# Hybrid attention and RWKV kernel, one core: attention of layer 0 interleaved with its z, u and output projections, values as matmul weights in two column halves, probabilities divided in place

## What is computed

```python
def _even_mixer(h, w_in, w_out, sgu_norm_g, sgu_w, sgu_b):
    B, S, _ = h.shape
    proj = h @ w_in
    q, k, v, u, z = jnp.split(proj, [WIDTH_A, 2 * WIDTH_A, 3 * WIDTH_A, 3 * WIDTH_A + WIDTH_B], axis=-1)
    heads = lambda t: t.reshape(B, S, N_HEADS_A, HEAD_DIM)
    o_a = _dilated_attention(heads(q), heads(k), heads(v)).reshape(B, S, WIDTH_A)
    o_b = _spatial_gating(u, z, sgu_norm_g, sgu_w, sgu_b)
    return jnp.concatenate([o_a, o_b], axis=-1) @ w_out
```

## Time and profile before

| | us |
|---|---|
| median of 3 runs (lowest to highest) | 1554.79 (1551.72 to 1555.05) |
| the profiled execution | 1548.98 |
| its span, first to last instruction | 1547.0 |
| TensorE busy | 1336.6 (86%) |
| VectorE busy | 671.6 (43%) |
| ScalarE busy | 357.6 (23%) |
| GpSimd busy | 254.8 (16%) |
| mean granted TensorE clock | 0.923 of full speed |

### The profile page before, as it was taken

The page is one execution under the profiler, slowest core; times in us unless marked ns, Lnnn a source line. Parts: engine busy times, 40 slices in busy tenths (PEclk is TensorE's granted clock), DMA queues, the critical chain, the costliest instruction groups (busy, mean ns, idle before and its releaser), DMA issues.

```text
span 1547.0 us, 23213 instructions
## 1 busy us (share of the span) xinstructions
PE 1336.6 (86%) x8816; PEld 811.9 (52%) x8816; DVE 671.6 (43%) x1373; ACT 357.6 (23%) x806; POOL 254.8 (16%) x263
## 2 busy tenths in 40 slices
PE   0899979997799994699999799999999895999990
PEld 0444557756344441343443688888887454444440
DVE  6426434564133233805026556666763324232324
ACT  1100035102111111101048433333332102211111
POOL 1000037000010012100001423444431200100102
PEclk9999867897899997799999899999997997899995
DMA  8649655373599995311110000000001313699975
GB/s 312 205 143 353 205 191 191 129 252 118 183 348 372 355 355 207 127 55 55 55 54 1 29 3 3 19 2 3 3 2 48 116 55 123 206 344 350 372 274 203
DMA packets 128997, 248.35 MB, mean 161 GB/s; under 512 B 8352, under 2 KB 78192, under 8 KB 128912
## 3 DMA queue, kind: packets, MB, share of 16 engines
q1 hardware_dynamic: 116816, 203.09, 37.9%
q0 software_dynamic: 7344, 26.74, 4.7%
q10 hardware_dynamic: 4752, 17.30, 2.7%
HBM read 219.33 MB, written 27.79 MB: 160 GB/s over the span
## 4 chain that ended last, share of the span: by engine, by line
PE 81%; DVE 8%; issue 4%; DMA 3%; ACT 2%; POOL 1%; POOLq 0%; DVEq 0%; SPq 0%; ACTq 0%
PE PS L1905 15%; PE PS L1723 11%; PE PS L1715 9%; PE PS L1922 7%; PE PS L1767 7%; PE PS L2049 2%; PE PS L2065 2%; PE PS L1894 2%; PE PS L2019 2%; PE PS L2071 2%; PE PS L1698 2%; PE PS L1954 2%; DMA arena<-in_ada_w 2%; PE PS L2104 1%; PE PS L1839 1%
## 5 line engine op out<-in xcount | busy, mean ns | idle before, releaser
L1905 PE MATMUL PS<-WR,arena 128*128 (+1 forms) x528 | 238.8, 606 | 11.3 <-ACT arena L1036 6.2
L1723 PE MATMUL PS<-arena,WR 128*128 128x512 f32 x384 | 168.0, 597 | 3.4 <-ACT arena L970 3.4
L1905 PEld LDWEIGHTS PS<-WR,arena 128*128 128x128 f32 x528 | 99.7, 194 | 128.5 <-issue 124.3
L1715 PE MATMUL PS<-WR,arena 128*128 128x512 f32 x320 | 143.1, 607 | 3.8 <-DVE arena L1478 3.8
L1723 PEld LDWEIGHTS PS<-arena,WR 128*128 128x128 f32 x384 | 73.3, 192 | 96.4 <-issue 92.8
L1922 PE MATMUL PS<-W,arena 128*128 x264 | 119.0, 593 | 3.9 <-DVE arena L1412 3.9
L1207 DVE SCALAR_TENSOR_TENSOR arena<-arena,cact 128x1024 f32<-128x1024 f32 x77 | 98.8, 1283 | 36.5 <-DMA arena<-in_ada_w 31.8
L1767 PE MATMUL PS<-WR,arena 128*128 128x512 f32 x256 | 112.2, 595 | 0.0
L1401 DVE TENSOR_TENSOR arena<-arena,PS 128x256 f32<-128x256 f32 x33 | 13.9, 421 | 212.1 <-ACT arena L1049 191.1
L1715 PEld LDWEIGHTS PS<-WR,arena 128*128 128x128 f32 x320 | 61.6, 195 | 83.2 <-issue 76.3
L796 POOL TENSOR_TENSOR LO<-GB,tmp 128x256 f32<-128x256 f32 x80 | 71.0, 906 | 100.6 <-DVE GB L1540 72.6
(11 more groups left out here) (321 smaller groups left out, 2062.3 us busy)
## 6 DMA issues: line engine op xcount, KB each, us to landing
WR<-in_moe_w SPq DMA_DIRECT2D x66, 1024.0 KB, 7.5
arena<-in_ada_w SPq DMA_DIRECT2D x96, 512.0 KB, 5.2
W<-in_moe_w SPq DMA_DIRECT2D x33, 1024.0 KB
expert_rows<-arena ACTq DMA_DIRECT2D x33, 512.0 KB, 7.2
WR<-in_rwkv_w_rkv SPq DMA_DIRECT2D x6, 2048.0 KB, 7.9
WR<-in_mix_w_in SPq DMA_DIRECT2D x5, 2048.0 KB, 10.6
WR<-in_mix_w_out SPq DMA_DIRECT2D x2, 2048.0 KB, 8.1
expert_rows<-arena SPq DMA_DIRECT2D x1, 4096.0 KB, 14.3
```

Of the source, the lines that this page charges most:

```text
L1715: last = mm(out, act_T[:, c, b * P:(b + 1) * P], WR[:, tile % 2, c, :], start=(c == 0), stop=(c == KC - 1))
L1723: last = mm(out, WR[:, tile % 2, c, f * P:(f + 1) * P], act_T[:, c, :], start=(c == 0), stop=(c == KC - 1))
L1905: last = mm(PS[:, 2, :], XgT[:, c, :], WR[:, slot, c, :].rearrange("p s f -> p (s f)"), start=(c == 0), stop=(c == KC - 1))
```

## The change

- **Order on TensorE.** z and u are no longer projected ahead of attention. One block of z comes ahead of the scores of rounds 0, 2, 4 and 6, one block of u ahead of those of rounds 8, 10, 12 and 14. Tiles are loaded in the order q, k, v, z, u. mod(2) is in round 6, the transposes of the gating weights in round 8, the mixing products in rounds 10 to 13, the transposes of their result in rounds 12 to 15. In round 16 come gate(0) and the first unit of the output projection, in round 17 the second, in round 18 mod(3); `out_proj` goes on from the third.
- **Values as weights.** A pair's output is now made with V as weights (64 columns) and the transposed probabilities as moving operand (128 columns), the even head on the lower half of the columns, the odd head on the upper. The result has features on partitions, so the transposes `oT` (L1857) and their copies are gone; VectorE copies the bank to `OT0` (in the area LO), and `sT` goes to `ST0`, where z was.
- **Divided in place.** VectorE makes the reciprocals of a pair's denominators one round later and multiplies the pair's two rows of probabilities by them before they are transposed.
- **Ada steps.** VectorE does 2 instead of 3 steps behind each block of v, one at the head of rounds 0 to 3, two in each of rounds 6 to 17, so all 24 of L = 2; GpSimd does none. SP loads the second output tile behind all chunks of L = 2.
- ScalarE's gelu (and the sum of z's squares) comes ahead of the exps of every even round.

```diff
+MOD2_AT, SWT_AT, MIX_AT = 6, 8, 10
...
-        tiles = [(io["mix_w_in"][0], n * 512) for n in range(5)] + [(io["mix_w_out"][0], n * 512) for n in range(2)]
-        tile_last = [("q", 3), ("k", 3), ("v", 3), ("u", 3), ("z", 3), ("y", 3), ("y", 7)]
+        tiles = [(io["mix_w_in"][0], n * 512) for n in (0, 1, 2, 4, 3)] + [(io["mix_w_out"][0], n * 512) for n in range(2)]
+        tile_last = [("q", 3), ("k", 3), ("v", 3), ("z", 3), ("u", 3), ("y", 3), ("y", 7)]
...
             tile(6)
-            for m in range(12, 3 * KC):
-                ada(2, m)
             sp.wait_ge(*free("u", 4))
             sp.wait_ge(*free("k", 4))
             sp.wait_ge(*free("q", 4))
@@ -670,7 +681,7 @@
                                  ).then_inc(M("w2_in"), 16)
 
...
-            for c in range(KC):
-
-                n = 2 * 3 * KC + 2 * KC + c
-                a, part = acc[:, 2 * D:3 * D], aring[:, n % 4, :]
-                gp.wait_ge(sem(f"ada_in{n % 4}"), 16 * (n // 4 + 1))
-                if c == 0:
-                    gp.wait_ge(*full("mod", 3))
-                    gp.wait_ge(sem("ada_step"), n)
-                    gp.tensor_scalar(a, part, cact[:, 0:1], None, ALU.mult).then_inc(sem("ada_step"), 1)
-                else:
-                    link(gp.tensor_scalar(part, part, cact[:, c:c + 1], None, ALU.mult))
-                    gp.wait_ge(sem("ada_step"), n)
-                    gp.tensor_tensor(a, a, part, ALU.add).then_inc(sem("ada_step"), 1)
 
...
-                               ).then_inc(drained["swT"], 1)
+            def gelu(n):
+
+                if n < NPAIR // 2:
+                    b = n // 2
+                    act.wait_ge(*full("z", b + 1))
+                    nc.scalar.activation(Z0[:, b, :], bank("z", b), ACT.Gelu).then_inc(drained["z"], 1)
+                    act.wait_ge(*free("z", b + 1))
+                    nc.scalar.activation(GB[:, 0:WA], Z0[:, b, :], ACT.Square, accum_out=ss[:, b:b + 1]
+                                         ).then_inc(sem("zss_ready"), 1)
+                else:
+                    b = n // 2 - NB
+                    act.wait_ge(*full("u", b + 1))
+                    nc.scalar.activation(U0[:, b, :], bank("u", b), ACT.Gelu).then_inc(drained["u"], 1)
+
             for n in range(NPAIR + 3):
+                if n < NPAIR and n % 2 == 0:
+                    gelu(n)
...
-                some_ada(3)
-            mod(2)
-            some_ada(12)
-
-            rms(1, sem("zss_ready"), 4, WA)
-            v.wait_ge(sem("gz_in"), 16)
+                some_ada(2)
 
             for n in range(NPAIR + 3):
-                if NB < n <= 2 * NB:
-                    b = n - NB - 1
+                if n < 4:
+                    some_ada(1)
+                if n == MOD2_AT:
+                    mod(2)
+                if n == MIX_AT - 2:
+                    rms(1, sem("zss_ready"), 4, WA)
+                    v.wait_ge(sem("gz_in"), 16)
+                if n == NPAIR - 1:
+                    diag(0, 0)
+                if 0 <= n - MIX_AT - 1 < NB:
+                    b = n - MIX_AT - 1
...
+                if 0 <= n - MIX_AT + 2 < NB:
+                    k = n - MIX_AT + 2
+                    stt(Z0[:, k, :], Z0[:, k, :], rstd[:, k:k + 1], gz, ALU.mult, ALU.mult).then_inc(sem("zn"), 1)
+                if MOD2_AT <= n < MOD2_AT + 3 * KC // 2:
+                    some_ada(2)
...
+                if 1 <= n <= NPAIR:
+                    i = (n - 1) // PPB
+                    k = 2 * (n - 1)
+                    two = slice(k % NHA, k % NHA + 2)
+                    v.wait_ge(sem("probs"), k + 2)
+                    link(nc.vector.reciprocal(rden[:, i % 2, two], den[:, i % 2, two]))
+                    for h in range(2):
+                        row = Pb[:, (k + h) % 6, 0:(i + 1) * P]
+                        ts(row, row, rden[:, i % 2, k % NHA + h:k % NHA + h + 1], None, ALU.mult
+                           ).then_inc(sem("rden"), 1)
                 if n >= 3 and (n - 3) % PPB == PPB - 1:
                     i = (n - 3) // PPB
-                    v.wait_ge(sem("probs"), NHA * (i + 1))
-                    nc.vector.reciprocal(rden[:, i % 2, :], den[:, i % 2, :]).then_inc(sem("rden"), 1)
-                    v.wait_ge(sem("rden"), i + 1)
                     v.wait_ge(sem("pv"), NHA * (i + 1))
-                    if i >= 2:
-                        v.wait_ge(*full("oT", i - 1))
-                    tt(OB[:, i % 2, :].rearrange("p (h d) -> p h d", h=NHA),
-                       bank("o", i).rearrange("p (h d) -> p h d", h=NHA),
-                       rden[:, i % 2, :].unsqueeze(2).to_broadcast([P, NHA, HD]), ALU.mult
-                       ).then_inc(drained["o"], 1)
-            del todo[0:8]
-            diag(0, 0)
+                    nc.vector.tensor_copy(OT0[:, i, :, :], bank("o", i).rearrange("p (c t) -> p c t", c=4)
+                                          ).then_inc(drained["o"], 1)
...
+                if n < NPAIR and n % 2 == 0:
+                    kind, b = ("z", n // 2) if n < NPAIR // 2 else ("u", n // 2 - NB)
+                    if b == 0:
+                        tile_ready(pe, 3 if kind == "z" else 4)
+                    rows(kind, b, b, 3 if kind == "z" else 4, HT)
+                if n == MOD2_AT:
+                    mod(2)
+                if n == SWT_AT:
+                    pe.wait_ge(sem("consts"), 10)
...
+                if n == 3:
+                    pe.wait_ge(*free("v", 4))
                 if n < NPAIR:
...
-                    if n == 0:
-                        pe.wait_ge(sem("zss_ready"), 4)
...
                         out = open_bank(pe, "pT", k)
-                        pe.wait_ge(sem("probs"), k + 1)
+                        pe.wait_ge(sem("rden"), k + 1)
...
-                    i = (n - 3) // PPB
-                    for k in (2 * n - 6, 2 * n - 5):
-                        h = k % NHA
-                        out = open_bank(pe, "o", i) if h == 0 else bank("o", i)
-                        pe.wait_ge(*free("pT", k + 1))
-                        for j in range(i + 1):
-                            last = mm(out[:, h * HD:(h + 1) * HD], PT[:, k % 4, j * P:(j + 1) * P],
-                                      V0[:, j, h * HD:(h + 1) * HD], start=(j == 0), stop=(j == i))
-                        last.then_inc(sem("pv"), 1)
-                if NB + 2 <= n < 2 * NB + 2:
-                    b = n - NB - 2
+                    i, pair = (n - 3) // PPB, (n - 3) % PPB
+                    out = open_bank(pe, "o", i) if pair == 0 else bank("o", i)
+                    pe.wait_ge(*free("pT", 2 * n - 4))
+                    for j in range(i + 1):
+                        for hh in range(2):
+                            k = 2 * n - 6 + hh
+                            h = k % NHA
+                            last = mm(out[hh * HD:(hh + 1) * HD, pair * P:(pair + 1) * P],
+                                      V0[:, j, h * HD:(h + 1) * HD], PT[:, k % 4, j * P:(j + 1) * P],
+                                      start=(j == 0), stop=(j == i))
+                    last.then_inc(sem("pv"), 2)
+                if 0 <= n - MIX_AT - 2 < NB:
+                    b = n - MIX_AT - 2
...
+                if n == NPAIR + 2:
+                    mod(3)
+                if NPAIR <= n < NPAIR + 2:
+                    b = n - NPAIR
+                    if b == 0:
+                        gate(0)
+                        tile_ready(pe, 5)
+                        pe.wait_ge(*free("sT", 4))
+                    pe.wait_ge(*free("o", b + 1))
+                    out_unit(0, 5, 0, b)
+            pe.wait_ge(*free("o", 4))
+            out_proj(0, 5, 2)
```

151 lines of the change are left out of this document (65 added, 86 removed).

## The result

| us | before | after |
|---|---|---|
| median of 20 executions each, in turns | 1552.26 | 1562.01 |
| lowest to highest | 1538.86 to 1555.11 | 1554.16 to 1570.10 |
| the profiled execution, its span | 1548.98, 1547.0 | 1569.27, 1566.3 |
| TensorE, VectorE, ScalarE busy | 1336.6, 671.6, 357.6 | 1337.6, 686.9, 372.7 |
| GpSimd busy | 254.8 | 214.5 |

The ratio after to before is 1.0075, 95% interval 1.0053 to 1.0096: slower by 11.6 us (8.2 to 14.9), where 6.8 were forecast.

A forecast was written before the change was run, and what follows sets the result against it. TensorE was taken as the bound (86% busy), with waits near attention's start and half-clock stretches. mod(3) 8.8 us later, less 2.0 afterwards, gave +6.8 on 1549.0; with 5.8 for the median, 1561.6 us, range 1547 to 1572.

The forecast's parts named there:

- work at full clock: TensorE's own work from the value projection to mod(3)'s end, priced at 2.4 GHz: 154.8 us.
- low clock: Time lost at half clock: 5.1 us after mod(2), 6.0 us in holes at the start, round 9, rounds 15 and 16.
- The forms: Price of values-as-weights products on TensorE: 10.7 us in all if the column halves overlap, 17.9 if not.
- Rival C: Column halves of the values-as-weights products don't overlap: 17.9 us for 10.7, +7.2, total 1568.8; chance 0.12.
- The start: Start of attention: TensorE waits 8.0 us before the third z unit, behind a late ada step, VectorE and ScalarE work.
- Waits of rounds 5 to 16: TensorE waits 16.6 us in these rounds, for copies behind a table load, VectorE's divides and late-emptied mixing banks.
- Rival B: VectorE isn't late in odd rounds; waits of rounds 5 to 16 and two clock falls vanish: 1541.3, half 1548; chance 0.20.
- Rival A: The clock holds through TensorE's holes: +0.8 us, total 1555.6; chance 0.18.
- Tables: ScalarE's gelu/exp switches: 16 loads of 1.28 us for 2, on the path only at the start (two) and round 5.
- rival D: A table switch costs another 1.28 us at three places on the path: +3.8, total 1565.4; chance 0.04.
- After mod(3): Moved output units gain nothing, as TensorE waits twice for VectorE; only waits for late output units fall away: -2.0 us.
- Sum: mod(3) ends 8.8 us later, less 2.0 afterwards: +6.8 on the profiled 1549.0, plus 5.8 to the median: 1561.6 us.

The follow-up runs named there:

- all rearrangements: Changed kernel with ada steps behind divides, mod(3) before second output unit, u tile and last L = 1 steps later, diagonals in round 9: 1543.95 and 1544.80 us.
- ada steps behind: Changed kernel with the two ada steps of rounds 6 to 17 behind the round's two divides instead of ahead of them: 1555.25 us.
- the start: Changed kernel with the last four L = 1 ada steps ending rounds 1 to 4 and the u tile loaded behind all L = 1 chunks: 1563.59 and 1559.39 us.
- mod(3) early: Changed kernel with mod(3) in round 17, and VectorE's mod(3) and six ada steps ahead of the last output copy: 1555.73 us.
- without gelu: Changed kernel with plain copies of u and z on ScalarE instead of gelu, so no table switches: 1557.04 us, one execution.
- write early: All rearrangements, with the 4 MB write moved to rounds 8 to 14 and the second output tile behind the fourth L = 3 chunk: 1539.60 us.

## Why the prediction was right, point by point

The forecast was 1561.6 us and the median 1562.01. Its mechanism is the one that the traces show, but two of its terms were off and nearly cancelled, and so were the two parts of its total.

| up to mod(3)'s end, us | forecast | measured |
|---|---|---|
| work at full clock | 154.8 | (taken as it is) |
| waits (start: gap less 1.5 of work) | 24.6 | 19.4 |
| low clock | 11.1 | 17.3 (the remainder) |
| sum, counted from the value projection | 190.5 | 191.5 |

The last column isn't cleaner than the forecast. 154.8 is the forecast's own sum, so any error in it lies in the remainder. One is visible: mod(2) and mod(3) were put at 7.9 us each as work at full clock, but the clock fell inside the rows that this was read from. mod(3) took 5.61 us with all rearrangements, at a clock of 0.94, and mod(2) 6.11 in the changed kernel's repeat, at 0.86. So some 4 us of low clock were hidden in the work, and low clock cost about 21 us where 15 were forecast.

- **The forms.** Values as weights were taken at 0.133 us a product and measured 0.128. Rival C (the full 0.224) is out: even one half after the other they take 0.19. The reason that I gave, overlap of the halves, is likely but not isolated. Changes of tiling show no gap in the rows.
- **The start.** The ada chunk behind the fourth weight tile landed at +41.2 (forecast +41.7), the gap between the z units was 8.9 us (9.5), the third unit came at +51.1 (+51.4). The working held to half a microsecond in this profile, and that was in part luck: in the repeat the chunk landed at +43.9, the gap was 11.6 and the unit came at +53.7, and in three edited kernels with the same start it came at +53.1 to +53.3 (first waits of 2.71 to 2.88 us). mod(3) came at +182.8 all the same, because TensorE lost 2.5 us less to the clock.
- **Waits of rounds 5 to 16.** Forecast 2.4, 1.3, 3.5, 0.7, 1.6, 2.2, 4.9; measured 1.68, 0.68, 3.11, none, 1.00, 1.27, 4.28. Each was too long by 0.4 to 0.9; I think that I put too much for the hops between the engines, which no experiment tests. Rival B (VectorE isn't late in odd rounds) is wrong by mechanism. Moving the steps made its case true in part and gave 9.5 us at mod(3), so its price was well founded.
- **The clock.** The mis-sized term. I had it fall after mod(2) and in three holes. It also fell from 177 to 181 behind round 5's wait of 1.68 us, and from 249 to 253 behind round 13's of 1.00. Four dense units took 0.65 to 2.3 us more than 6.88 (5.8 in all, where I had 2.1 for each), rounds 6 and 7 doubled from 3.0 to 6.1. (The prediction also has it at 0.50 until 4.3 us after mod(2); by its own rows that is 176 - 171.78 = 4.2.) Rival A (the clock holds) is out.
- **Tables.** The loads count where I had them, the gap behind a load is 0.02 us, and without the two loads at the start 2.7 us of waits went, 1.35 for each, so rival D (a second 1.28 for each) is out. The Trainium skill, page "ScalarE: Activation LUTs", section "What ACT_TABLE_LOAD costs", states a drain of 1.38 us on top; no row here shows it.
- **After mod(3).** The two waits are there, 7.27 and 3.21 us, and the gain of the units that moved forward is gone. I took -2.0 for this stretch. Between mod(3)'s end (9.8 later) and the transposes of x (8.2 later) it was -1.6, and by the means of two profiles each (10.7 and 8.7 later) -2.0.
- **Sum.** The stage came out 8.2 us later against the profile that I worked from (6.8 forecast) and 9.4 by the means of two profiles each. The total is 10 to 12 us slower. The forecast of the total was closer than that of its stage because the 5.8 us that I added for the distance between the profiled execution and the median of three runs was too much: the median of 20 lay 3.3 above it. By the medians of 20 the changed kernel is 9.8 us slower, 3.0 more than forecast, and the base was 2.5 below the median that I started from; that the two nearly cancelled was luck.

## What to carry to other kernels

When independent work is put between the steps of a chain (score, minimum, exp, divide, transpose), its place within the round decides. In round 9 the two ada steps (2.6 us) ahead of the divides made TensorE wait 2.6 us longer than behind them; in round 16, where other work also stood ahead, 1.3. Here these steps on the wrong side of two divides cost the stage nearly as much as the whole change lost. After each gain, read what ends the next wait: here it went from VectorE's order to a 4 MB write and a 2 MB tile that stood ahead of needed chunks, and then to VectorE's own work.

A change of several parts is worth splitting. One part of this one shortened the stage by 5 to 7 us, the rest lengthened it by 15.

## What the runs showed of the hardware

- Behind a small wait the clock can fall, but the same wait doesn't always bring it: behind the wait of 1.00 us in round 13 the granted clock was 0.57 from 249 to 253 us, the same as behind the 4.28 us of round 16. From round 13's transposes (249.34) to the next dense unit (252.97) it was 3.6 us, where the same three groups took 2.1 in round 12 (243.23 to 245.38). Ten of the profiles have this wait of 1.00 us in front of the same work. In five (the changed kernel twice, ada steps behind, the start twice) the three groups took 3.4 to 3.6 us, in five (mod(3) early, without gelu, all rearrangements twice, write early) 2.1. Round 5's wait of 1.60 to 1.68 us was followed by a dense unit of 8.83 us in five profiles and of 7.13 in five, one of each from the changed kernel and one of each from "the start". Round 13 without a fall, repeat of all rearrangements:

```profile
235.87 2.00 PE L1841 MATMUL PS<-arena 128*128 128x64 f32 x16 [1.00 <-DVE tmp L1339]
237.70 0.82 PE L1850 MATMUL PS<-ident,arena 128*128 128x128 f32 x6
...
239.76 7.03 PE L1726 MATMUL PS<-WR,arena 128*128 128x512 f32 x16
```

- fp32 products with 64 columns of weights and 128 moving columns: 0.128 us each with the column halves in turns, 0.19 with one half after the other (one execution).
- Code that no edit touched, from layer 1's projections on, took 912.4 and 906.9 us in two executions of one kernel, and 911.9 and 919.0 in two of another. A stage's marks, not the total, are what tells edits of a few microseconds apart.
